# Block two's output and routing woven into the first gathers, and the gate columns woven into a projection

## The reference, cut to what matters

```python
# PEER, for token n, head h, pick k, with index e = idx[n, h, k]
w = gelu(dot(h_tok[n], u[e])) * softmax_k(score[n, h])[k]
out[n] += w * v[e]
```

## Time and profile before

| | before |
|---|---|
| median of 3 runs | 1620.18 us (1619.58 to 1621.11) |
| the profiled execution | 1622.18 us, its span 1620.4 us |
| PE, PE weight load, DVE busy | 90%, 49%, 49% of the span |
| ACT, POOL busy | 18%, 19% |
| bytes from HBM | 548 MB, 339 GB/s over the span |

### The profile page before, as it was taken

How to read it: one execution, slowest core, us unless ns; L and a number is a source line. 1 busy time by engine, 2 the same in 40 slices (tenths; PEclk the granted TensorE clock), 3 DMA queues, 4 the chain that set the end, 5 groups by cost and what they waited for, 6 DMA issues and landing times.

```text
span 1620.4 us, 16884 instructions
## 1 busy us (share of the span) xinstructions
PE 1456.6 (90%) x6246; PEld 789.7 (49%) x6246; DVE 787.2 (49%) x1864; ACT 289.6 (18%) x702; POOL 311.4 (19%) x291
## 2 busy tenths in 40 slices
PE   7999999899999999999999888889788777877778
PEld 5887875544444444444546655555333333333333
DVE  2256645332232322322524558465767576757544
ACT  1422431100000000000243222122122111111111
POOL 0001000100000000000000024353564444444441
PEclk9999999999999999999999989999998999899999
DMA  9642456399999999999625058999999999999997
GB/s 361 272 151 104 157 205 263 107 431 428 426 429 428 427 428 427 425 426 428 282 96 223 7 185 357 394 422 407 392 422 421 421 421 421 422 421 421 421 422 290
DMA packets 60371, 550.58 MB, mean 340 GB/s; under 512 B 8704, under 2 KB 8992, under 8 KB 10368
## 3 DMA queue, kind: packets, MB, share of 16 engines
q1 hardware_dynamic: 22336, 277.47, 41.4%
q0 software_dynamic: 37952, 271.99, 41.0%
HBM read 548.39 MB, written 1.05 MB: 339 GB/s over the span
## 4 chain that ended last, share of the span: by engine, by line
PE 49%; DMA 38%; issue 5%; DVE 5%; ACT 2%; POOL 1%; SPq 0%; DVEq 0%; POOLq 0%; ACTq 0%
DMA ring<-expert_w_d 17%; DMA ring<-peer_uv_d,work 14%; PE ps L1830 10%; PE ps L1598 8%; PE ps L1195 7%; DMA mod<-peer_uv_d,work 5%; PE ps L1678 4%; PE ps L1189 4%; PE ps L1314 3%; PE ps L1473 2%; PE ps L1203 1%; PE ps L1639 1%; PE ps L1553 1%; PE ps L1320 1%; POOL ring L1978 1%
## 5 line engine op out<-in xcount | busy, mean ns | idle before, releaser
L1830 PE MATMUL ps<-ring,work 128*128 128x512 f32 x728 | 354.4, 630 | 76.4 <-ACT work L1135 76.3
L2921 DVE CUSTOM_DVE_ANT_0 ring<-ring,work 128x1024 f32<-128x1024 f32 x182 | 222.2, 1222 | 120.0 <-DMA ring<-peer_uv_d,work 118.3
L1830 PEld LDWEIGHTS ps<-ring,work 128*128 128x128 f32 x728 | 141.9, 200 | 267.4 <-issue 165.9
L1978 POOL DMA_INDIRECT ring<-peer_uv_d,work x182 | 199.1, 1094 | 245.7 <-PE ps L1830 166.1
L1598 PE MATMUL ps<-ring,work 128*64 128x512 f32 x1024 | 225.6, 593 | 10.0 <-DMA ring<-expert_w_d 9.1
L1598 PEld LDWEIGHTS ps<-ring,work 128*64 128x64 f32 x1024 | 78.4, 137 | 154.0 <-issue 153.0
L1135 ACT ACTIVATE work<-consts_sb,work 128x128 f32<-128x128 f32 x256 | 85.1, 392 | 251.0 <-DVE work L2930 239.4
L1195 PE MATMUL ps<-ring,hT 128*128 128x512 f32 (+1 forms) x288 | 119.3, 571 | 1.7 <-ACT hT L996 0.8
L1830 PE MATMUL ps<-work 128*128 128x512 f32 x148 | 83.5, 693 | 35.5 <-ACT work L1135 35.5
L1639 PE MATMUL ps<-ring,work 128*64 128x512 f32 x512 | 113.4, 595 | 0.7 <-DVE work L2486 0.7
L2482 DVE TENSOR_TENSOR work<-work,ps 128x512 f32<-128x512 f32 x16 | 11.0, 687 | 198.7 <-PE ps L1598 198.7
(11 more groups left out here) (417 smaller groups left out, 1652.2 us busy)
## 6 DMA issues: line engine op xcount, KB each, us to landing
ring<-expert_w_d SPq DMA_DIRECT2D x96, 2048.0 KB, 15.7
ring<-w_ada_d SPq DMA_DIRECT2D x12, 2048.0 KB, 7.9
ring<-w_in_d SPq DMA_DIRECT2D x12, 2048.0 KB, 17.5
ring<-w_out_d SPq DMA_DIRECT2D x4, 2048.0 KB, 7.7
ring<-peer_w_query_d SPq DMA_DIRECT2D x4, 2048.0 KB, 8.3
ring<-peer_uv_d,work POOLq DMA_INDIRECT x182, 23.3
ring<-w_in_d SPq DMA_DIRECT2D x2, 1024.0 KB, 22.9
mod<-b_ada_d SPq DMA_DIRECT2D x1, 2048.0 KB, 23.2
```

The source lines that it names most:

```text
L1830: last = pe.matmul(ps[V_BANK[t] + n][:, :], diag[:, i % 4, :], v_row(i)[:, n * 512:(n + 1) * 512], start=(i % (16 * PH) == 0), stop=(i % ( ...
L1978: pool.indirect_dma_start(out=uv_rows(i), out_offset=None, in_=io["peer_uv"], in_offset=bass.IndirectOffsetOnAxis(ap=idx[:, s, k:k + 1], a ...
L2921: dve.tensor_tensor_reduce(out=u_row(i), in0=u_row(i), in1=h_tok[:, i // (16 * PH), :], scale=1.0, scalar=0.0, op0=ALU.mult, op1=ALU.add, ...
```

## The change

It has these parts:

- **The start.** `modulation(3)` moves ahead of the last quarter of the keys' first half, `warm(10)` becomes `warm(5)`, and the gate columns are no longer a block of their own: after each matmul of `q0` comes one of the gates. `q0` is then taken ahead of the gates by DVE and ACT.
- **Fillers.** `warm` is issued at five places of tile 1's block two, into the upper one of tile 0's value banks.
- **Head 0 first.** `q00` is taken by DVE and no longer by ACT. DVE does parts 5 to 21 of head 0's route ahead of `moba_out(1)`, and head 1's parts later, between the dots.
- **Half a query later.** PE does two parts of `q01` ahead of `yT1`, the other two after `wo11`; its scores come after values 4 and 5.
- **Values in the output.** DVE's first dots stand between the output's additions; values 4 and 5 stand ahead of `sc01` and `xT1`. The late queries begin at value 6, each with ten values (`FIRST = 6`).
- **A 17th place**, the memory of tile 1's turned probabilities, free after `o1`. It is used for gathers 1 and 7 only.
- `EARLY`, the pick up to which a batch has two picks, goes from 64 to 72. Route 1's parts run two to a pick from pick 10 to 22, before 3 in 2 picks from pick 7 to 23.

```diff
+FIRST = 6
-    done = {q: 2 * (STEPS * j + 4) for j, q in enumerate(LATE_QUERIES)}
-    steps = [("q00", (13,)), ("go11", (12,)), ("yT10", (14,)), ("wo10", (0, 1)), 2, ("wo11", (2, 3)), ("row", (15,))]
+    done = {q: FIRST + 2 * (STEPS * j + 4) for j, q in enumerate(LATE_QUERIES)}
+    steps = [("q00", (13,)), ("o1", (16,)), ("go11", (12,)), ("yT10", (14,)), ("wo10", (0, 1)), 2, ("wo11", (2, 3)), 4,
+             ("row", (15,)), FIRST]
-UV_PLACES = 16
-EARLY = 64
+UV_PLACES = 17
+EARLY = 72
...
             key_chunk(7, 2 * P, 0, 0)
+            modulation(3)
             key_chunk(7, 3 * P, T, 0)
-            modulation(3)
             columns(1)
-            warm(10)
+            warm(5)
...
+            for c in range(2):
+                for k in range(KC):
+                    last = pe.matmul(b[:, c * T:(c + 1) * T], wt[:, k, c * P:(c + 1) * P], hT[:, k, :],
+                                     start=(k == 0), stop=(k == KC - 1))
+                    side = pe.matmul(gates[:, 16 * c:16 * c + 16], hT[:, k, c * P:(c + 1) * P], tail_w[:, k, 0:16],
+                                     start=(k == 0), stop=(k == KC - 1))
...
             gla_keys(1)
+            warm(4, V_BANK[0] + 1)
             key_scores(0, 0)
             gla_scores(1)
+            warm(6, V_BANK[0] + 1)
             moba_turned(1)
             gla_state(2)
+            warm(6, V_BANK[0] + 1)
             moba_values(1)
             gla_values(1)
-            query(0, 1)
-            key_scores(0, 1)
+            query_part(0, 1, 0)
+            query_part(0, 1, 1)
             pe.wait_ge(tok_ready, 3)
             to_features("yT", 1, y2)
+            warm(4, V_BANK[0] + 1)
             out_projected(1, 0)
             values(0, 2)
             out_projected(1, 1)
             values(2, 4)
+            query_part(0, 1, 2)
+            query_part(0, 1, 3)
+            values(4, FIRST)
+            key_scores(0, 1)
             pe.wait_ge(tok_ready, 4)
             to_features("xT", 1, x)
...
             routes(0, 2, 5, 0)
             turned_p(1, 0)
             turned_p(1, 2)
-            routes(0, 5, 11, 0)
+            routes(0, 5, 8, 0)
             gla_state(2)
+            routes(0, 8, 22, 0)
             moba_out(1)
-            routes(0, 11, 22, 0)
+            routes(0, 0, 3, 1)
             gla_out(1)
-            routes(0, 0, 5, 1)
+            routes(0, 3, 5, 1)
             features_in("yT", 1, 1)
-            routes(0, 22, PARTS, 0)
-            routes(0, 5, 12, 1)
...
+            dot(0)
+            routes(0, 22, PARTS, 0)
+            dot(1)
+            routes(0, 5, 7, 1)
+            weights(0)
+            dot(2)
+            out_added(1, 0)
+            dot(3)
+            routes(0, 7, 10, 1)
+            weights(1)
+            dot(4)
+            routes(0, 10, 22, 1)
+            dot(5)
+            out_added(1, 1)
+            squares(1, 5)
+            weights(2)
+            dot(6)
+            row_normed()
+            dot(7)
+            routes(0, 22, PARTS, 1)
```

More of the change, by code:

```diff
@@ L306, in uv_plan @@
         if isinstance(step, int):
-            for i in range(v, min(step, n - UV_PLACES)):
-                plan.append((plan[i][0], None, i + 1))
+            for i in range(v, step):
+                if len(plan) < n and (plan[i][0] != 16 or i < 2):
+                    plan.append((plan[i][0], None, i + 1))
             v = step
@@ L1106, in _ @@
             moba_exps(1)
-            query(0, 0)
             states_in(1)
@@ L1136, in applied @@
                                        scale=w_cur[:, s, k:k + 1]).then_inc(diag_ready, 1)
-            for h in range(2):
-                exp_gates(gates[:, 0, h, :], h + 1)
+            exp_gates(gates[:, 0, 0, :], 1)
             applied(0, 4)
+            exp_gates(gates[:, 0, 1, :], 2)
+            applied(4, FIRST)
             root(5)
+            query(0, 1)
+            key_scores(0, 1)
             features_in("xT", 1, cols2)
-            at = 4
+            at = FIRST
             for j, (t, g) in enumerate(LATE_QUERIES):
-                turn = 2 * (STEPS * j + 4)
+                turn = FIRST + 2 * (STEPS * j + 4)
                 applied(at, turn)
@@ L2970, in _ @@
             for b, (i, size) in enumerate(PICKS):
-                e_ = i if size == 1 else i + size if size == 2 else min(i + size + 1, n_picks - 8)
-                weights_after.setdefault(e_, []).append(b)
-            first_parts = [(0, part, 1) for part in range(12, PARTS)]
-            next_parts = [(1, part, None) for part in range(PARTS)]
-            for i in range(n_picks):
-                dot(i)
+                if i >= FIRST:
+                    e_ = i if size == 1 else i + size if size == 2 else min(i + size + 1, n_picks - 8)
+                    weights_after.setdefault(e_, []).append(b)
+            dot(0)
[18 more added lines that the diff above has]
+            routes(0, 22, PARTS, 1)
+            for i in range(FIRST, n_picks):
+                if i >= 8:
+                    dot(i)
                 for b in weights_after.get(i, ()):
                     weights(b)
-                if i == 2:
-                    out_added(1, 0)
-                if i == 4:
-                    out_added(1, 1)
-                    squares(1, 5)
+                if i == 8:
                     scaled_in("xT", 1, cols2)
@@ L2986, in _ @@
                     assert bt[0] == len(b_mine)
[L2987 to L2994 removed]
+                if 10 <= i < 23:
+                    routes(1, 2 * (i - 10), min(2 * (i - 10) + 2, PARTS))
                 elif i >= 32:
```

62 lines of the change are left out of this document (28 added, 34 removed).

## The result

The changed kernel takes 1607.86 us (median of 4 runs, 1604.22 to 1609.11), the kernel before 1620.64 in the same comparison (4 runs, 1619.58 to 1621.85): ratio 0.9899, 95% interval 0.9876 to 0.9921. That is 12.8 us less; 13.5 were forecast, and 1606.7 us. Timed once more later, beside the kernel before, it took 1604.93 (6 runs, 1602.13 to 1614.81), ratio 0.9878 [0.9854, 0.9902]. The profiled execution has a span of 1607.1 us and a time of 1608.94.

A forecast was written before the change was run, and what follows sets the result against it. It took PE and DMA as matched, the end set by how many gathers have landed when the DMA's full stretch starts. Block two's 10.9 plus the start's 2.6 us made 13.5 off 1620.18: 1606.7 us, range 1600 to 1614.

The forecast's parts named there:

- Block two: Tile 1's block two: six gathers more under way give 14.9 us, less 4.0 for a later `q10`: gain 10.9 us.
- D: How much later `q10` begins in tile 1's block two than before: 3.5 us, taken as 4.0.
- The two products: Tile 1's two value products on PE: 8.7 us at full clock, bounds 8.7 and 12.4.
- The largest step: From the value products through tile 1's finished, turned row to the output: `wo10` at 936.0 instead of 946.73, 10.7 us.
- Value 6: Start of the first late query: PE waits 3.3 us (bounds 2.9 and 4.6), then 5.4 for the pair from half clock.
- The start: Kernel's start: 0.75 us at `columns(1)` plus 1.9 from woven gate columns, rounded to 2.6 (bounds -1.6 and 6).
- The 1.7 for the clock: At the start, `q0` ran 4 us at clock 0.57 behind the gate columns; weaving them keeps the clock, saving 1.7 us.
- The clock falls anyway: Rival, 912 to 929 us: the clock still falls, value products keep 12.4 us, time 1610.4; chance 0.22.
- The dips go too: Rival: the DMA runs through 1034 to 1048 and 1160 to 1180, 4.7 us more gained, time 1602; chance 0.10.
- DVE takes over: Rival, DVE's route parts and picks: each of 13 picks 0.4 us late, 5.2 in all, time 1612; chance 0.12.
- Slower: Rival, weights in DVE's queue: over 1.3 us late for each of 13 picks, time 1624 and more; chance 0.03.
- nothing: Rival: the DMA alone sets the end, block two gains nothing, only the start's 2.6 us remain, time 1617.6; chance 0.03.

The follow-up runs named there:

- e2: The changed kernel with the start of the kernel before, so block two's edits only: 1611.54 us, ratio 0.9906 to the kernel before.
- e4: The changed kernel with ten fillers at the start instead of five: 1608.52 us, ratio 0.9883 to the kernel before.
- e6: The changed kernel with twenty fillers added ahead of value 150: 1608.34 us, ratio 0.9903 to the kernel before.
- e5: The changed kernel with twenty fillers added ahead of the third pair of values in the first late query: 1611.50 us, ratio 0.9925 to the kernel before.
- e7: The changed kernel with each query part ahead of its two values in the first late query: 1604.39 us, ratio 0.9883 to the kernel before.
- e10: The changed kernel with `EARLY` back from 72 to 64: 1604.79 us, ratio 0.9884 to the kernel before.
- e11: The changed kernel with all four parts of `q01` ahead of `yT1`: 1613.16 us, ratio 0.9933 to the kernel before.
- e12: The changed kernel without any edit, timed once more: 1604.93 us, ratio 0.9878 to the kernel before.
- e3: The changed kernel without its four calls of fillers in block two: 1612.72 us, ratio 0.9925 to the kernel before.
- e8: The changed kernel without the 17th place, so with sixteen: 1610.90 us, ratio 0.9914 to the kernel before.
- e9: The changed kernel with the first late query's parts ahead of their values and ten fillers at the start: 1604.20 us, ratio 0.9877 to the kernel before.

## Why the prediction was right, step by step

**Block two, 10.9 forecast, 10.9 in the pair, 7.9 to 14.6 over five profiles of it** (the changed kernel twice, e2, e4 and e6, whose fillers cost nothing). Counting PE's schedule and a plan shifted by six held: POOL is six gathers ahead at the last scores (81 and 75), and the end moves with PE's schedule ahead of them (e5, e7) and not with PE's work behind (e6). That the pair gives the forecast to 0.1 us is luck, as the 7.9 to 14.6 show. The stretch behind the last scores became 476.8 - 460.4 = 16.4 us shorter, where 6 x 2.49 = 14.9 were counted; since the same kernel gave 463.5 the second time, which makes 13.3, the 1.5 between them is no term of its own. D was 98.3 - 94.5 = 3.8 at `q10` (4.0 forecast) and 5.5 at the last scores; in four profiles whose clock did not fall at the last step of the first late query (e2, e4, e6, e10) it was 1.0 to 1.5 at `q10`. Single steps, the forecast's less the 2.6 us of the start:

1. The value product at 917.9: it came at 917.80, without a wait.
2. The two products 8.7 us: 7.8 (917.80 to 925.57), at full clock. The forecast was 0.9 too high in the second product, which took 4.2 us and not 5.0: four of its short records in a row take 0.64 us, and it was scaled from pairs, which take 0.42.
3. `wo10` at 933.4: 932.74. The largest step, 10.7 us, is right to 0.7. PE did wait for `yT1`, 1.41 us. e11 fills this wait, and pays for it elsewhere.
4. 29.7 us of PE from `wo10` to `xT1`'s end without a wait: 932.74 to 962.35, 29.6. The dots of gathers 4 and 5 ended at 947.4 and 953.3, where 947.4 and 954.4 were due; gather 0 left at 926.27.
5. Value 6 at 966.4 behind a wait of 3.3 us: 965.57, 3.22. The half clock took 6.4 for the pair (to 971.97) and not 5.4 (6.3 in e12); e2, e4, e6 and e10 have 5.1 to 5.2.
6. `q10` at 1000.0: 1000.52. The clock fell a second time, at 991.50. The 12.6 us taken over for this piece from the query before have such a fall in them (3.54 behind a wait of 2.90 at 1023.13), so it was counted without being named; from the last part to `q10` 12.9 were measured (987.63 to 1000.52). Where no fall comes there, as in e2, e4, e6 and e10, the forecast is 1.7 too long.

What D still grew behind `q10`, from 3.8 to 5.5, lies in the third late query, where no step of mine looked. PE there in the kernel before, then in the changed kernel, and ACT in the changed kernel at the first of the two waits:

```profile
1082.39 3.70 PE L1830 MATMUL ps<-ring,work 128*128 128x512 f32 x8 [1.49 <-ACT work L1135]
...
1088.61 1.98 PE L1830 MATMUL ps<-work 128*128 128x512 f32 x4 [1.63 <-ACT work L1135]
```

```profile
1082.20 3.67 PE L1839 MATMUL ps<-ring,work 128*128 128x512 f32 x8 [2.70 <-ACT work L1135]
...
1089.81 5.40 PE L1839 MATMUL ps<-ring,work 128*128 128x512 f32 x8 [3.05 <-ACT work L1135]
```

```profile
1080.02 0.20 ACT L1126 ACTIVATE work<-work 128x2 f32<-128x2 f32 x1
1080.24 1.28 ACT L1118 ACT_TABLE_LOAD   x1
1081.53 0.23 ACT L1118 ACTIVATE work<-work 128x32 f32<-128x32 f32 x1
1081.67 0.68 ACT L1135 ACTIVATE work<-consts_sb,work 128x128 f32<-128x128 f32 x2
```

The exponentials of a route (`L1118`, 32 numbers wide) stand between a batch's GELU (`L1126`) and its diagonals (`L1135`), with a table load of 1.28 us; the next batch's GELU pays another to load its own back. Before, this came three batches later (ACT's load at 1093.30), where PE had no wait; with the plan shifted by six it falls on the batches at the end of the query, which PE does wait for. That is 1.2 and 1.4 us of wait and 1.7 of half clock more, 4.3 (the half clock came in both profiles of this kernel and not in e3, e6, e7 and e10), against 2.9 saved at the wait that stood at 1023.13 before (1.57 after, and no half clock), and 0.3 of small ones. Moving that route's part by one batch was not tried. The Trainium skill, "ScalarE: Activation LUTs", section What ACT_TABLE_LOAD costs, gives 2.66 us for a switch, 1.28 for the load and the rest for a drain; the load's row agrees, but from the GELU's end at 1080.22 to the exponentials' start only 1.31 us pass, so the drain is not paid here.

**The start, 2.6 forecast, 0.1 in the pair: the step that failed.** Two of its terms were wrong. For `columns(1)` 0.75 were counted: 1.95 became 1.84, as the row's own records, and no copy, filled it. With the five fillers less, the stretch from the columns to the keys went from 4.12 us (35.66 to 39.78) to 3.64 (36.02 to 39.66), so 0.5; in this pair the columns began 0.36 later, which took most of it back. The 1.7 for the clock was counted as if the woven gates alone decided it. They do keep it (50 to 54 at 1.00), but with five fillers dropped and a wait of 0.57 the fall can come at 40 us, ahead of them, and takes the same 1.7 back. The weave itself is worth nothing: a pair of a long and a short matmul takes 0.655 us, and 16 of them 10.4 (48.28 to 58.68), as much as 3.6 for the gates and 6.9 for `q0` at full clock apart. By the Trainium skill, "TensorE: Matmul & The Clock Gate", Part 2, weight loads can be pulled ahead of the running matmul; had that hidden them all, the gates would by the prediction's estimate have been nearly free (3 us more). The rows show no such gain. Counted from the columns' first record, the start gives 0.4 to 0.5 us with the fall and 2.1 without it.

**The 2.3 us that I did not forecast** made up for the start in the pair of profiles. They are the clock over 304 to 312 (0.79 before, 1.00 after), in code that is the same; e12 has 0.72 there. That the sum came so close is partly this chance. Over ten runs of the changed kernel the median is 1606.7.

**The 17th place, counted 0, is worth 3.8 us at `q10` and at the last scores in e8's profile.** I looked at whether PE waits for gather 1; what counts is that with a place more the fourth gather leaves before `wo10`, and what is queued behind its dot on DVE. By the timed medians e8 is 3.0 above the changed kernel of the first comparison, which ran on another chip; by itself that is not beyond the spread.

**`EARLY`, counted 0, is 0 as far as e10 can tell.**

**The rivals.** *The clock falls anyway*: no, in every profile of block two with the fillers it was 1.00 over 912 to 934. The turned probabilities, a row of 16 transposes at 913.89, stand between the fillers, and the fall did not come. The rule that I weighed here, that a transpose does not count as PE-busy in the same way (the Trainium skill, "TensorE: Matmul & The Clock Gate", Part 4), does not decide this stretch; with fillers on both sides of them no run isolates the transposes. What the fall would have cost was also mis-sized: the 12.4 us were read from a stretch at 0.58, and at 0.50 the products take 14.3; with the parts of `q01` behind them e3 pays 7.3 us at `wo10` and not 3.7. *The dips go too*: the one at 1034 is gone (419 GB/s), that at 1160 not quite (398), but 990 to 1034 now moves less (355 against 419 GB/s), and 1120 to 1140 too (369 against 388), so nothing is won. *DVE takes over*: over 1000 to 1010 it is busy 8.80 of 10, and the weights' waits that grew are ACT's table loads. *Slower* and *nothing*: no. The DMA alone does not set the end, as e7 shows, and e5 by the estimate above.

## What to carry to other kernels

Where a stretch that waits for data follows one that computes, find the last point where the computing engine decides how many transfers are under way, and count its schedule to that point; what is behind it costs nothing (e6), what is ahead of it is paid one to one (e5, by the estimate). A buffer more is judged by what stands in the queue behind the transfer that it frees, not by who waits for that transfer (e8). And before a step of a few microseconds is credited to a change, profile the same kernel twice, and count the half clocks behind each wait: they can hide a stall of the same size (e5).

## What the runs showed of the hardware that I had not expected

- TensorE's clock is not decided by the program alone. Behind the same wait of 2.76 us two values took 3.70 us in e7 and 5.40 in e9; behind 0.57 us the keys took 7.17 or 8.78 us in two profiles of one program. Each such fall costs 1.5 to 1.7 us (2.9 at value 6 of the changed kernel), and the router's stretch, which no kernel here changed, put the first expert's matmul between 307.2 and 314.3 us. That this is most of the spread of the timed runs is likely and not shown; of the ten runs of the changed kernel the slowest (1614.81) has the lowest mean granted clock, 0.968.
- Behind a long stretch at 1.2 GHz (e3, 922 to 934 and `q01` to 938) the next two waits of 3.22 and 1.92 us brought no fall, where they did in the changed kernel; but they brought none either in e5, whose clock was 1.00 over all of 912 to 990, so the long stretch need not be the reason.
- The DMA moved 421 or 422 GB/s over 1180 to 1580 us in all 14 profiles, with PE busy between 308 and 321 us of the 400.
